# Nine convolution taps on the vector engine, memory rows turned inside the convolution, three steps in another order, and the eight lightest experts four to a round

## The chip, the cores and the metric

The kernel runs as one launch on one core of a Trainium2 chip. The time is device time in microseconds (us) of that core. The five engines (TensorE, VectorE, ScalarE, GpSimd, SyncE) run programs of their own and meet only at semaphores. In the profile's words they are PE (PEld is its weight load), DVE, ACT, POOL and SP; a q behind a name is the engine's queue of DMA issues.

## The reference

One inference step of a decoder layer for 512 prompt rows and 8 sample rows (T = 520 tokens, D = 1024), in float32:

```python
z = rms_norm(x, norm_g) @ w_in                  # 1024 -> 2048: gMLP u, v | conv a, b
a_out = gelu(u) * chunk_spatial_mix(layer_norm(gelu(v)), gm_ws, gm_bs)
glu = cv_a * sigmoid(cv_b)                      # 512 channels
conv = depthwise_causal_conv(glu, conv_w)       # 31 taps
b_out = silu(layer_norm(conv + conv_b))
x = x + concat(a_out, b_out) @ w_out
k, v = rms_norm(mem) @ wk, rms_norm(mem) @ wv   # 256 memory rows, 4 heads
x = x + softmax(q k^T / 16) v @ wo              # q = rms_norm(x) @ wq
...
xt = rms_norm(x)
g = argmax(xt @ router_g + b)                   # top-1 of 4 groups
e = top_2(xt @ router_e[g] + b)                 # top-2 of its 8 experts
out = sum over both of w_e * ((silu(xt @ w1[e]) * (xt @ w3[e])) @ w2[e])
y = rms_norm(x + out)
```

Every expert holds three float32 matrices of 1 MiB each (1024x256, 1024x256, 256x1024).

## The kernel before, in words

It is one function with a hand-written program for each engine. All order is in the code: lists such as `STREAM` (weight loads), `MM_ORDER`, `TV_ORDER` and `TA_ORDER` (who gets the PSUM buffers next) and counting semaphores.

**Dense part.** Activations lie transposed (channels on partitions). A weight slice of 256 columns is loaded by SP into one of four 1 MiB buffers, ScalarE copies it to a rounded high part (`split_h`, L694), VectorE subtracts to a low part (`split_l`, L996), and `project` (L1588 to L1590) makes each product from three matmuls: high x high, low x high, high x low. Two slices' parts fit, so slice n waits for the matmuls of slice n-2. The two PSUM buffers `mm` alternate; a block is free again when VectorE or ScalarE has read it (`mm_used`). The order is: turn x (L1584), 16 blocks of `w_in`, turn the memory rows, the convolution, 8 blocks of keys (`wk`) and 8 of values (`wv`) with the spatial mixing and the layer norm of the convolution between them, 8 of `w_out`, 8 of queries with attention, `wo`, routing.

**Head.** ScalarE scales xT into xH (L715, per k), VectorE makes xL (`moving_l`, L1035), then ScalarE squares the token rows (L720), and through `tok_ms`, a root and `diag` TensorE makes the row of token norms `rs0`, `rs1` (L1645), placed behind block 1. VectorE needs them (`rstd`, L1050) before it can read blocks 0 and 1 out of PSUM (L1095).

**Convolution.** The 512 channels lie as 4 x 128; `conv_taps` (L1694) does all 31 taps on TensorE as 32x32 matmuls with diagonal weights `dw`, 16 for a tap. Ahead of it four groups of memory rows are turned (`mem0` to `mem3`, L1584); each must be read by ScalarE (L752) and VectorE (L1130) before the group two later can be turned, and the taps come last. Behind it ScalarE adds the bias (L770) after it has waited for `m_mean`, the memory norm that VectorE makes once its layer norm of v (L1138) is done.

**Norms between blocks.** `mean(n)` takes two sums out of PSUM (L1007), waits for ScalarE's root, and does a reciprocal (L1009). In the keys the split of slice 11 stands behind `mean(0)` and the scaling of the convolution (L1199); in the queries the split of slice 21 stands behind `mean(1)` and the scaling of the router.

**Experts.** VectorE ranks the 32 experts by their number of rows. Places 0 to 5 are fixed experts, the others follow rank. A round gathers 128 slots (`xe`, GpSimd), turns them, does `hidden` (L1978) with w1 and w3, and `down` (L2006) with w2. A round holds one expert with 128 slots (S) or two with 64 (P), each writing its own rows of PSUM. 28 places lie in 16 fixed rounds; at least one pass of a loop does two more P rounds (places 28 to 31). Weights of an expert go into one of `RING` = 7 slots; SP loads place p+7 into the slot of p: gate and up (L580) after `hid_ready` of p's round, down (L584) after its `y_done`. The down weights of a round are queued ahead of the gates of the next.

## Time and profile before

| | |
|---|---|
| median of 3 runs | 739.23 us (738.95 to 741.88) |
| the profiled execution | 738.92 us, span 737.2 us (1.7 us lie around the span) |
| PE busy | 644.9 us (87%), PEld 471.3 us |
| DVE / ACT / POOL busy | 299.9 / 208.6 / 81.7 us |
| moved by DMA | 179.4 MB, 243 GB/s in the mean |

Busy shares are means over stages that differ much; what holds a stage up is read from the chain of waits and from the timeline of that stage. In the timeline a number in brackets is the idle time ahead of an instruction, with the one that ended it.

### The profile page before, as it was taken

Reading aid. Unit: us, or ns where it says so; the run is one execution under the profiler, and the core shown is the slowest. Engines: PE = TensorE matmul, PEld = TensorE weight load, DVE = VectorE, ACT = ScalarE, POOL = GpSimd, SP = SyncE. Lnnn points to the kernel's source line nnn. Section 1 sums busy time; section 2 is a strip of 40 time slices with the busy share of each in tenths; the row PEclk is TensorE's granted clock in tenths of the full one; section 3 lists DMA queues with packets and bytes.
Section 4 is the critical chain, followed back from the end, with each engine's and each line's share of the span. In section 5 each row is a group of like instructions: output and inputs, shape, how many; then the busy total and the mean of one; then the engine's idle time right before and its main releaser. Section 6 shows DMA issues by size and latency. Waiting matters only on the chain.

```text
span 737.2 us, 11996 instructions
## 1 busy us (share of the span) xinstructions
PE 644.9 (87%) x4939; PEld 471.3 (64%) x4939; DVE 299.9 (41%) x598; ACT 208.6 (28%) x359; POOL 81.7 (11%) x117
## 2 busy tenths in 40 slices
PE   3899997999899998999899996699999999999720
PEld 3899997668799998996678875234333343433210
DVE  3644655808653445578722237111212121121138
ACT  4711423114643433436202132111112121121122
POOL 0000000600000220100101110112121211111100
PEclk8899999999999999999998996699999999999965
DMA  9823130303375432378984649699999999999553
GB/s 289 253 68 135 64 109 1 118 4 90 131 193 141 160 116 91 140 247 291 350 295 190 228 164 418 254 415 420 421 420 419 421 418 419 417 416 417 234 215 142
DMA packets 75470, 179.42 MB, mean 243 GB/s; under 512 B 9710, under 2 KB 56490, under 8 KB 62088
## 3 DMA queue, kind: packets, MB, share of 16 engines
q1 hardware_dynamic: 65868, 163.47, 59.2%
q0 software_dynamic: 6176, 12.76, 4.7%
q10 hardware_dynamic: 3372, 2.42, 1.0%
q8 instruction: 39, 0.64, 0.4%
q14 instruction: 15, 0.12, 0.0%
HBM read 173.85 MB, written 16.66 MB: 258 GB/s over the span
## 4 chain that ended last, share of the span: by engine, by line
PE 75%; DMA 9%; DVE 8%; issue 4%; ACT 2%; SPq 1%; ACTq 1%; DVEq 0%; POOLq 0%
PE ps L1978 15%; PE ps L1588 12%; PE ps L1590 12%; PE ps L1589 12%; PE ps L2006 7%; PE ps L1694 4%; DMA w<-exp_w 4%; PE ps L1584 4%; PE ps L1775 2%; DMA raw<-cache_mem_k 2%; PE ps L1875 1%; DMA xs_rows<-x_sample 1%; PE ps L1712 1%; PE ps L1837 1%; DVE rstd L1009 1%
## 5 line engine op out<-in xcount | busy, mean ns | idle before, releaser
L1588 PE MATMUL ps<-xH,w_h 128*128 128x260 f32 x512 | 150.0, 293 | 9.2 <-DVE xL L1035 5.2
L1589 PE MATMUL ps<-xH,w_l 128*128 128x260 f32 x512 | 146.7, 286 | 0.0
L1590 PE MATMUL ps<-xL,w_h 128*128 128x260 f32 x512 | 146.7, 286 | 0.0
L1978 PE MATMUL ps<-w,xeT 128*64 128x512 f32 (+1 forms) x512 | 129.0, 601 | 3.9 <-DMA w<-exp_w 2.6
L1588 PEld LDWEIGHTS ps<-xH,w_h 128*128 128x128 f32 x512 | 98.7, 193 | 14.6 <-DVE w_l L996 7.7
L1978 PEld LDWEIGHTS ps<-w,xeT 128*64 128x64 f32 (+1 forms) x512 | 44.6, 145 | 86.1 <-issue 84.4
L1589 PEld LDWEIGHTS ps<-xH,w_l 128*128 128x128 f32 x512 | 98.7, 193 | 0.3 <-issue 0.2
L1590 PEld LDWEIGHTS ps<-xL,w_h 128*128 128x128 f32 x512 | 98.6, 193 | 0.0
L996 DVE TENSOR_TENSOR w_l<-raw,w_h 128x2048 fp32r<-128x2048 f32 x28 | 64.1, 2289 | 35.3 <-ACT w_h L694 35.3
L2006 PE MATMUL ps<-w,aT 128*64 128x512 f32 (+1 forms) x256 | 66.0, 599 | 10.5 <-DVE aT L1501 10.5
L694 ACT ACTIVATE w_h<-raw 128x2048 fp32r<-128x2048 f32 x28 | 53.3, 1904 | 19.1 <-PE ps L1590 17.6
L1494 DVE SCALAR_TENSOR_TENSOR gated<-ps,rs_slot,silu 128x256 f32<-128x256 f32 x16 | 7.7, 484 | 111.4 <-ACT silu L935 111.4
L2006 PEld LDWEIGHTS ps<-w,aT 128*64 128x64 f32 (+1 forms) x256 | 20.8, 143 | 43.5 <-issue 30.4
L1588 PE MATMUL ps<-w_h,xH 128*128 128x256 f32 x128 | 37.4, 292 | 4.1 <-DVE w_l L996 3.1
L1508 DVE COPY ye<-ps 128x512 f32<-128x512 f32 x18 | 12.5, 692 | 68.0 <-PE ps L2006 68.0
L935 ACT ACTIVATE silu<-ps,rs_slot 128x256 f32<-128x256 f32 x16 | 7.6, 475 | 102.9 <-PE ps L1978 102.9
L1590 PE MATMUL ps<-w_l,xH 128*128 128x256 f32 x128 | 36.7, 287 | 0.0
L1589 PE MATMUL ps<-w_h,xL 128*128 128x256 f32 x128 | 36.5, 285 | 0.0
L1590 PE MATMUL ps<-cL,w_h 128*128 128x260 f32 x128 | 36.2, 283 | 0.0
L1588 PE MATMUL ps<-cH,w_h 128*128 128x260 f32 x128 | 36.1, 282 | 0.0
L1589 PE MATMUL ps<-cH,w_l 128*128 128x260 f32 x128 | 36.1, 282 | 0.0
L2125 POOL DMA_INDIRECT y_rows<-ye,ids x16 | 16.1, 1009 | 172.6 <-DVE ye L1508 172.6
(332 smaller groups left out, 899.3 us busy)
## 6 DMA issues: line engine op xcount, KB each, us to landing
w<-exp_w SPq DMA_DIRECT2D x96, 1024.0 KB, 21.4
raw<-w_in SPq DMA_DIRECT2D x8, 1024.0 KB, 6.7
raw<-cache_mem_k SPq DMA_DIRECT2D x8, 1024.0 KB, 6.6
raw<-cache_mem_v SPq DMA_DIRECT2D x8, 1024.0 KB, 11.9
raw<-xa_wk SPq DMA_DIRECT2D x4, 1024.0 KB, 5.7
raw<-xa_wv SPq DMA_DIRECT2D x4, 1024.0 KB, 5.4
raw<-xa_wq SPq DMA_DIRECT2D x4, 1024.0 KB, 5.1
raw<-xa_wo SPq DMA_DIRECT2D x4, 1024.0 KB, 5.5
```

The lines of the kernel that those rows point to most:

```text
L694: act.activation(w_h[n % 2][:], slot[:], ACT.Copy).then_inc(h_ready, 1)
L996: dve.tensor_tensor(w_l[n % 2][:], slot[:], w_h[n % 2][:].bitcast(F32), ALU.subtract).then_inc(l_ready, 1)
L1508: dve.tensor_copy(ye[j][:, 512:D], mm[1][:, 1, :]).then_inc(yv_ready, 1)
L1584: return pe.transpose(out, src, ident[0:n, 0:n])
L1588: pe.matmul(out, h1, h2, start=start, stop=False)
L1589: pe.matmul(out, l1, h2, start=False, stop=False)
L1590: return pe.matmul(out, h1, l2, start=False, stop=stop)
L1694: last = pe.matmul(out[r // 2][c * BAND:(c + 1) * BAND, r % 2, :], dw[c // 2][rows, c % 2, k, :], glu[rows, c, k:k + SEQ], start=k == 0, s ...
L1775: last = pe.matmul(out[:, j // 2, (j % 2) * MEM:(j % 2 + 1) * MEM], qT[:, 2 * h + kk, j * P:(j + 1) * P], kT[:, 2 * h + kk, :], start=kk = ...
L1978: last = pe.matmul(mm[0][half, j, :], xeT[j][:, k, half], w13[s][:, :, k, :], start=k == 0, stop=k == KT_D - 1)
L2006: last = pe.matmul(mm[1][half, b, :], aT[:, k, half], w2s[s][:, k, c], start=k == 0, stop=k == 1)
L2125: pool.indirect_dma_start(out=y_rows, out_offset=bass.IndirectOffsetOnAxis(ap=index, axis=0), in_=ye[j][:], in_offset=None, bounds_check=2 ...
```

## The change

Four things. (1) `V_TAPS` = 9 of the 31 taps become 36 VectorE instructions (`part_taps`), dealt out between its steps of `w_in` by `PART_AT` and between the memory rows; TensorE does 22 taps and adds VectorE's partial sum by 16 matmuls with the identity. `mem0` and `mem1` are turned ahead of the taps, `mem2` and `mem3` before the 7th and the 9th tap of TensorE. (2) The token squares go between the copies of x on ScalarE (three) and to VectorE (two); blocks 0 and 1 of `w_in` become one `first_pair` in three passes (high x high as xH comes, low x high, the norm rows, high x low); x is loaded by half, with a semaphore each. (3) The splits of slices 11 and 21 stand ahead of the waits for the root, the router's scaling behind the split of slice 22. (4) The rounds are `PPPSPPPSPQSPQS`: two rounds hold four experts with 32 slots each, 14 fixed rounds instead of 16. The step from rank to slot is written anew for three sizes. The number of experts loaded stays 32: by the reference's routing no expert is over its slots in either version (the eight lightest ranked ones have at most 24 rows).

```diff
-for kind in "PPPSPPSPPSPPSPPP":
+for kind in "PPPSPPPSPQSPQS":
     p = ROUNDS[-1][-1] + 1 if ROUNDS else 0
-    ROUNDS.append((p,) if kind == "S" else (p, p + 1))
+    ROUNDS.append(tuple(range(p, p + {"S": 1, "P": 2, "Q": 4}[kind])))
...
+                if j < 3:
+                    row = x_row(act, j)
+                    act.wait_ge(*((tok_sq, j) if j else (dve_made, 4)))
+                    act.activation(mem_junk[:], row, ACT.Square, accum_out=tok_ss[:, j:j + 1]).then_inc(tok_sq, 1)
...
+                dve.tensor_tensor_reduce(v_junk[0:n], row, row, 1.0, 0.0, ALU.mult, ALU.add,
+                                         tok_ss[0:n, j:j + 1]).then_inc(tok_sq_v, 1)
...
+                if n == 0:
+                    split_l(11)
                 dve.wait_ge(rs_root, n + 1)
                 dve.reciprocal(rstd[:], rstd[:]).then_inc(rs_ready, 1)
...
+            part_todo = [(k, c) for pair in ((0, 1), (2, 3)) for k in range(V_TAPS) for c in pair]
...
+                    src, w = glu[:, c, k:k + SEQ], cols_b[:, k, c:c + 1]
+                    if k == 0:
+                        ins = dve.tensor_scalar(conv[:, c, 0:SEQ], src, w, None, ALU.mult)
+                    else:
+                        dve.wait_ge(part_done, part_last[c])
+                        ins = dve.scalar_tensor_tensor(conv[:, c, 0:SEQ], src, w, conv[:, c, 0:SEQ], ALU.mult, ALU.add)
...
+            PART_AT = {4: 3, 5: 4, 6: 4, 7: 3, 8: 2, 9: 3, 10: 3, 11: 3, 14: 3}
...
             moving_l(7, 32, "xa_g")
+            split_l(21)
             mean(1)
...
+            def first_pair():
+
+                outs = [open_mm(("w_in", m)) for m in range(2)]
...
+                for k in range(8):
+                    pe.wait_ge(xh_ready, k + 1)
+                    for out, c in zip(outs, cols):
+                        for b, tok in enumerate(toks):
+                            pe.matmul(out[:, b, 0:HT], wh[:, k, c], xH[:, k, tok], start=k == 0, stop=False)
+                pe.wait_ge(l_ready, 1)
...
+                token_norms()
...
+            MEM_AT = {V_TAPS + 6: 2, V_TAPS + 8: 3}
...
-                for k in range(TAPS):
+                for k in range(V_TAPS, TAPS):
+                    if k in MEM_AT:
+                        mem_turned(MEM_AT[k])
+                    if k == TAPS - 1:
+                        pe.wait_ge(part_done, 4 * V_TAPS)
+                        for r in range(4):
+                            rows = slice(r * BAND, (r + 1) * BAND)
+                            for c in range(4):
+                                pe.matmul(out[r // 2][c * BAND:(c + 1) * BAND, r % 2, :], ident[rows, rows],
+                                          conv[rows, c, 0:SEQ], start=False, stop=False)
```

What VectorE does at the head, before, behind its copies of x (`w_l_55` is the low part of slice 0, `w_l_56` of slice 1):

```order
L1026 MEMSET glu 128x4x30
L996 TENSOR_TENSOR w_l_55<-raw_51,w_h_53 128x2048
L1035 SCALAR_TENSOR_TENSOR xL<-xT,cols_a,xH 128x520 x8
L1041 TENSOR_SCALAR tok_ss<-tok_ss 128x5
L1043 RECIPROCAL tok_ss<-tok_ss 128x5
L1046 TENSOR_SCALAR diag<-ident,tok_ss 128x128 x4
L1046 TENSOR_SCALAR diag<-ident,tok_ss 8x8
L996 TENSOR_TENSOR w_l_56<-raw_52,w_h_54 128x2048
L1050 COPY rstd<-ps 128x260 x2
```

And now, from the second of its two squares on:

```order
L1059 ISA v_junk,tok_ss<-xs_rows 8x1024
L1059 ISA tok_ss 8x1
L1063 TENSOR_SCALAR tok_ss<-tok_ss 128x5
L1019 TENSOR_TENSOR w_l_55<-raw_51,w_h_53 128x2048
L1072 SCALAR_TENSOR_TENSOR xL<-xT,cols_a,xH 128x520 x5
L1078 RECIPROCAL tok_ss<-tok_ss 128x5
L1081 TENSOR_SCALAR diag<-ident,tok_ss 128x128 x4
L1081 TENSOR_SCALAR diag<-ident,tok_ss 8x8
L1072 SCALAR_TENSOR_TENSOR xL<-xT,cols_a,xH 128x520 x3
L1086 COPY rstd<-ps 128x260 x2
L1019 TENSOR_TENSOR w_l_56<-raw_52,w_h_54 128x2048
```

The norm's reciprocal and `diag` moved between the fifth and the sixth xL, and the split of slice 1 behind the norm rows.

TensorE at the start of the convolution, before (`raw_51` holds the memory rows, 16 turns are the four groups):

```order
L1590 MATMUL ps<-xL,w_h_54 128x260
L1584 MATMUL ps<-ident,raw_51 128x128 x16
L1694 MATMUL ps<-glu,dw_109 32x512 x2
L1694 MATMUL ps<-glu,dw_110 32x512 x2
L1694 MATMUL ps<-glu,dw_109 32x512 x2
```

Now, at the 9th of TensorE's taps, where `mem3` is turned (8 turns stand ahead of the first tap, 4 more ahead of the 7th):

```order
L1794 MATMUL ps<-glu,dw_109 32x512 x2
L1794 MATMUL ps<-glu,dw_110 32x512 x2
L1641 MATMUL ps<-ident,raw_51 128x128 x4
L1794 MATMUL ps<-glu,dw_109 32x512 x2
L1794 MATMUL ps<-glu,dw_110 32x512 x2
```

The taps no longer stand behind the last group of memory rows.

VectorE in the keys, before (`w_l_56` is slice 11):

```order
L1152 COPY kT<-ps 128x512
L1007 TENSOR_SCALAR rstd<-ps 128x260 x2
L1009 RECIPROCAL rstd<-rstd 128x520
L1199 TENSOR_TENSOR cLf<-cLf,rstd 128x2080
L996 TENSOR_TENSOR w_l_56<-raw_51,w_h_54 128x2048
L1152 COPY kT<-ps 128x512
L996 TENSOR_TENSOR w_l_55<-raw_52,w_h_53 128x2048
```

And now:

```order
L1211 COPY kT<-ps 128x512
L1030 TENSOR_SCALAR rstd<-ps 128x260 x2
L1019 TENSOR_TENSOR w_l_56<-raw_51,w_h_54 128x2048
L1034 RECIPROCAL rstd<-rstd 128x520
L1259 TENSOR_TENSOR cLf<-cLf,rstd 128x2080
L1211 COPY kT<-ps 128x512
L1019 TENSOR_TENSOR w_l_55<-raw_52,w_h_53 128x2048
```

The split of slice 11 moved ahead of the reciprocal; slice 12 kept its place.

## Rows read from the trace of the kernel before

**Rows 1.** The page, the span in 40 slices of 18.43 us: bytes moved.

```profile
GB/s 289 253 68 135 64 109 1 118 4 90 131 193 141 160 116 91 140 247 291 350 295 190 228 164 418 254 415 420 421 420 419 421 418 419 417 416 417 234 215 142
```

**Rows 2.** Windows table: busy us of each engine, then clock, DMA share, GB/s.

```profile
60.00:100.00 40.00, 40.00 (x337) 39.96 (x336) 20.77 (x27) 12.41 (x12) 0.00 (x0) 1.00 0.23 80
```

**Rows 3.** The chain that ended last, expert stage: start, us, what.

```profile
468.63 8.67 PE ps L1978 x32
...
483.15 6.87 PE ps L1978 x32
...
649.75 6.89 PE ps L1978 x32
...
659.27 31.71 DMA w<-exp_w
...
691.12 7.10 PE ps L1978 x32
```

**Rows 4.** Timeline of SyncE's queue: start, us to issue, line, count.

```profile
477.49 2.10 SPq L580 DMA_DIRECT2D w<-exp_w  x4
...
579.87 6.54 SPq L580 DMA_DIRECT2D w<-exp_w  x4
...
656.88 8.62 SPq L580 DMA_DIRECT2D w<-exp_w  x4
```

**Rows 5.** Groups by form: partitions x elements, count, busy us, mean ns.

```profile
L1694 PE MATMUL ps<-glu,dw 32*32 32x512 f32 x992 | 33.3, 612 | 0.1
...
L1035 DVE SCALAR_TENSOR_TENSOR xL<-xT,cols_a,xH 128x520 fp32r<-128x520 f32 x16 | 11.8, 775 | 0.1
...
L1837 PE MATMUL ps<-raw,s_pT 128*32 128x256 f32 x128 | 7.1, 380 | 0.0
```

**Rows 6.** Timeline of the head: start, us, engine, line, idle before it.

```profile
15.79 5.05 ACT L715 ACTIVATE xH<-xT,cols_a 128x520 fp32r<-128x520 f32 x8
...
19.03 0.56 PE L1588 MATMUL ps<-xH,w_h 128*128 128x260 f32 x1 [5.17 <-DVE xL L1035]
...
24.37 0.42 PE L1588 MATMUL ps<-xH,w_h 128*128 128x260 f32 x1
...
24.89 0.28 PE L1588 MATMUL ps<-xH,w_h 128*128 128x260 f32 x1
...
36.08 0.36 PE L1588 MATMUL ps<-xH,w_h 128*128 128x260 f32 x1 [1.35 <-DVE glu L1095]
```

**Rows 7.** Timeline of TensorE, from the last input block to the first tap.

```profile
121.86 1.04 PE L1584 MATMUL ps<-ident,raw 128*128 128x128 f32 x8
126.78 1.90 PE L1584 MATMUL ps<-ident,raw 128*128 128x128 f32 x8 [3.88 <-DVE xL L1130]
128.61 1.16 PE L1694 MATMUL ps<-glu,dw 32*32 32x512 f32 x16
```

**Rows 8.** Timeline of the convolution's end and the first key block.

```profile
144.39 0.20 ACT L761 ACTIVATE m_ss<-m_ss 128x2 f32<-128x2 f32 x1 [12.62 <-DVE m_ss L1143]
...
161.99 2.66 ACT L770 ACTIVATE cLf<-ps,cols_a 128x512 f32<-128x512 f32 x4 [17.39 <-PE ps L1694]
...
163.44 0.36 PE L1588 MATMUL ps<-w_h,xH 128*128 128x256 f32 x1 [0.98 <-ACTq L775]
```

**Rows 9.** Timeline of the keys: split, first block behind it, copies of ScalarE.

```profile
195.01 2.29 DVE L996 TENSOR_TENSOR w_l<-raw,w_h 128x2048 fp32r<-128x2048 f32 x1
...
197.35 0.39 PE L1588 MATMUL ps<-w_h,xH 128*128 128x256 f32 x1 [3.08 <-DVE w_l L996]
...
200.33 2.20 ACT L796 ACTIVATE cH<-cLf 128x520 fp32r<-128x520 f32 x4
```

**Rows 10.** Timeline of the queries, TensorE alone.

```profile
289.03 0.36 PE L1588 MATMUL ps<-xH,w_h 128*128 128x260 f32 x1 [2.29 <-DVE cHf L1225]
```

**Rows 11.** Timeline of VectorE in the routing.

```profile
447.68 0.24 DVE L1399 TENSOR_SCALAR at_rank<-ps,part_no 32x32 f32<-32x32 f32 x1 [0.52 <-PE ps L1937]
...
453.04 0.18 DVE L1436 CAST slot_f<-slot_i 128x20 f32<-128x20 int32 x1
```

More of the change, by code:

```diff
@@ L42 @@
 PAST = TAPS - 1
+V_TAPS = 9
+PE_TAPS = TAPS - V_TAPS
 MEM = 256
@@ L82, in runs_of @@
     while at < len(values):
-        n = 1
-        while at + n < len(values) and values[at + n] == values[at] + n:
+        n, step = 1, values[at + 1] - values[at] if at + 1 < len(values) else 0
+        while at + n < len(values) and values[at + n] == values[at + n - 1] + step:
             n += 1
-        out.append((at, n, values[at]))
+        out.append((at, n, values[at], step))
         at += n
+    return out
     return out
@@ L376, in trunk_kernel @@
         rs_root = sem("rs_root")
+        x_landed = [sem(f"x_landed{j}") for j in range(NT - 1)]
         tok_sq = sem("tok_sq")
+        tok_sq_v = sem("tok_sq_v")
         tok_ms = sem("tok_ms")
@@ L537, in load @@
                         sp.dma_start(dst[g * BAND:(g + 1) * BAND, 4:8, :], rows).then_inc(landed[HOME[c]], 16)
+                elif kind == "x":
+                    for t in range(2):
+                        sp.dma_start(dst[:, t:t + 1, :], src[:, t:t + 1, :]).then_inc(x_landed[2 * i + t], 16)
                 else:
@@ L1432, in _ @@
[L1432 to L1435 removed]
+            dve.wait_ge(block_ready, 1)
+            link(dve.tensor_copy(first[:], mm[1][:, 0, 0:2 * EXPERTS]))
+            cap_b = each(first[:, EXPERTS:2 * EXPERTS]).broadcast_to([P, NT, EXPERTS])
@@ new lines, in _ @@
+            link(dve.tensor_tensor(ptmp[:], ptmp[:], each(first[:, 0:EXPERTS]).broadcast_to([P, NT, EXPERTS]), ALU.add))
+            link(dve.tensor_tensor(ptmp[:], ptmp[:], e_all[:].rearrange("p t g e -> p t (g e)"), ALU.add))
+            for_two = ptmp[:].rearrange("p (o t) e -> p o t e", o=1).broadcast_to([P, 2, NT, EXPERTS])
+            link(dve.tensor_tensor(wtmp[:], who[:], for_two, ALU.mult))
+            link(dve.tensor_reduce(place[:], wtmp[:], AX_X, ALU.add))
+            link(dve.tensor_scalar(place_i[:], place[:], float(OVER_FIRST), None, ALU.add))
@@ new lines, in first_pair @@
+            def first_pair():
+                outs = [open_mm(("w_in", m)) for m in range(2)]
+                wh = w_h[0][:].rearrange("p (k c) -> p k c", k=8)
+                wl = w_l[0][:].rearrange("p (k c) -> p k c", k=8)
+                cols = [slice(m * P, (m + 1) * P) for m in range(2)]
+                toks = [slice(b * HT, (b + 1) * HT) for b in range(2)]
+                pe.wait_ge(h_ready, 1)
+                for k in range(8):
[4 more added lines that the diff above has]
+                pe.wait_ge(l_ready, 1)
+                for out, c in zip(outs, cols):
+                    for k in range(8):
+                        for b, tok in enumerate(toks):
+                            pe.matmul(out[:, b, 0:HT], wl[:, k, c], xH[:, k, tok], start=False, stop=False)
+                token_norms()
+                for out, c in zip(outs, cols):
+                    for k in range(8):
+                        pe.wait_ge(xl_ready, k + 1)
+                        for b, tok in enumerate(toks):
+                            last = pe.matmul(out[:, b, 0:HT], wh[:, k, c], xL[:, k, tok], start=False, stop=k == 7)
+                    last.then_inc(mm_ready, 1)
@@ L1648, in _ @@
+            first_pair()
+            for m in range(2, 16):
+                project("w_in", m, xH, xL)
                 if m == 3:
@@ L1674, in _, with mem_turned @@
                         last.then_inc(tv_ready, 1)
-            slot = raw_in(pe, ("mem", 0))
-            for i in range(4):
+            def mem_turned(i):
+                slot = raw_in(pe, ("mem", 0))
                 out = open_tv(f"mem{i}")
```

180 lines of the change are left out of this document (99 added, 81 removed).

## The prediction, made before the changed kernel ran

> **What bounds the kernel now.** I read the chain of waits first, then the bytes by slice, SyncE's queue, and the timeline where TensorE waits. Two stages with different limits show.
>
> Up to the routing TensorE is the limit: nearly every piece of the chain there is its own, and what it does not do, or what it stops waiting for, comes off the time. Its waits are few: at the head it starts the first products at 19.03 and block 2 at 36.08 [rows 6]; between the last block of `w_in` and the first tap lie 128.61 - 121.86 = 6.7 us [rows 7]; one split in the keys costs 3.08 us of idling [rows 9], one in the queries 2.29 us [rows 10].
>
> From the second half of the routing on, the limit is the stream of expert weights. The first seven experts fill the slots; slot 0 is free again when the first `hidden` ends, and SyncE issues at 477.49 [rows 4]. From there the bytes stand at 415 to 421 GB/s in every slice up to 676 us [rows 1], and SyncE's issues stretch from 2.10 to 6.54 and 8.62 us for four [rows 4], as they do when a queue takes no more. TensorE runs beside it: from 483.15 to 649.75 lie 13 rounds, 12.8 us each [rows 3]. The last gate and up weights land at 659.27 + 31.71 = 690.98 and the last `hidden` starts at 691.12 [rows 3]; at TensorE's own pace that round would have come 649.75 + 3 x 12.8 = 688.2. So rounds and bytes are nearly in balance, and the bytes end last.
>
> **The change, part by part.** All on the clock of before; a step that ends earlier moves everything behind it, since nothing behind has a time of its own.
>
> *Head.* ScalarE's xH starts at 15.79, one k every 0.63 us (5.05 / 8) [rows 6]. The first pass of the pair needs only that: it starts at about 16.6 instead of 19.03. It has 32 matmuls. At 24.37 the rows still last 0.42, at 24.89 0.28 us [rows 6]: the granted clock went from 1.2 to 2.4 GHz 5.6 us after the start, and starts go from 0.22 to 0.12 us apart. Started at 16.6 it would change at 22.2: 26 matmuls by then, 6 more to 22.9; the second pass of 32 to 26.8, the norm rows (12 starts at 0.12 us, 1.4) to 28.2, the third pass to 32.1. VectorE's list: squares of two row tiles (1024 columns, an estimate of 1.3 us each from 520 in 0.775 [rows 5]), split of slice 0, five xL, reciprocal and `diag` near 24, three xL by 26.2, norm rows at 28.7, split of slice 1 to 31.0, block 0 read at 31.7. So block 2 starts at 32.1 instead of 36.08: **-4.0**. Bounds: -1.5 if the squares between ScalarE's copies push xH by a us and the split of slice 1 comes late too; -5.5 if the clock rises sooner.
>
> *Taps.* 31 taps take 33.3 us [rows 5], 1.07 each: nine less are -9.6. The partial sum's 16 matmuls have a tap's form: +1.1. The taps start behind `mem1`, at 122.9 (121.86 + 1.04 [rows 7]), instead of 128.61, and the 8 later turns (0.9) stay between them: -4.8. The end comes then at 148.4, and ScalarE's bias is not held by the taps alone any more. It waits for `m_mean`, which came at 144.39 in a VectorE list that started behind `mem3` [rows 8]. `mem3` is now turned behind eight taps, by 132.3 instead of 128.68, and partial taps stand among the groups, so `m_mean` comes some 4.3 us later, near 148.7: +0.3. Sum **-13.0** for the start of the keys (163.44 [rows 8]). Bounds: -9 (a VectorE list 4 us later than I have it) and -13.5.
>
> VectorE pays 36 x about 0.62 us (a 520-column instruction of this kind lasts 0.775 and the next starts before it ends [rows 5]) = 22 us. It is busy 20.77 of 40 us in `w_in` [rows 2]; from block 4 to block 15 are some 60 us, so 29 are free, for 28 instructions (17 us). I went through the list block by block: with four taps in a block the next split ends 7.0 us behind the block, its successor is wanted 11.5 behind. Hidden, price 0. If that cover were gone, each us that VectorE is late costs TensorE one.
>
> The GPSIMD Engine Reference of the Trainium skill (1. Specifications) says that GpSimd shares its memory interfaces with VectorE when an instruction there has two inputs in SBUF, as these have. It would hurt under GpSimd's work; here GpSimd is busy 0.00 us [rows 2], so the rule has no hold.
>
> The turns inside the taps are another matter: the array goes from 32x32 tiles to whole and back twice. At the one such change of before, turns end at 128.68 (126.78 + 1.90) and the first tap starts at 128.61 [rows 7]: nothing lost. The Trainium skill, TensorEngine Tiling (Array Packing), Key Properties, says that changing the mode drains the engine; with a drain as long as a tap's matmul (0.612 us [rows 5], an estimate) four changes are 2.4 us and the time would be 721.1. I go by the row.
>
> *Keys.* Slice 11's split (195.01 to 197.30 [rows 9]) stands before the reciprocal and ends near 191; its block starts at 194.4 instead of 197.35. But ScalarE is busy for the convolution until 200.33 + 2.20 = 202.5 [rows 9], so block wk6 is read out at 203.0 and wv0 starts there, against 205.3 before: **-2.2**. Bounds: 0 (TensorE idles 2.5 us there and falls back to half clock) and -4.5.
>
> *Queries.* Slice 21 is split while the norm is made; queries 0 are read right after the reciprocal, block 2 starts at about 286.7 instead of 289.03 [rows 10]: **-2.3**, bounds -1 and -2.5. The router's scaling (under 0.5 us) lies before queries 2, TensorE in a block.
>
> *Routing.* From `at_rank` to `slot_f` are 453.04 - 447.68 = 5.4 us, some 25 small instructions [rows 11]. The new text has fewer in a row, but three of 160 columns: I add up 5.0, **-0.5**, bounds -1.2 and +0.5. GpSimd writes 33 instead of 18 runs of the tables, 19 us before they are read: 0.
>
> *Rounds.* 73 loads of 1 MiB land from 477.49 to 690.98: 2.92 us each. The first `hidden` is as it was, so the stream starts, and the last gate lands, at the same place of this clock. With 67 loads the gates of 28 and 29 are in at 673.4; with 56 those of 26, at 641.3; with 37 those of 19, at 585.7, where the first group of four is due. Fewer rounds only make TensorE wait: some 17 us before the second group (the round ahead of it ends at 624.1), 4.9 us before the last round (673.4 + 12.8 = 686.2 to 691.0). The freed slots are asked for 17 us and more before the stream gets to them, so it has no hole. **0** for the two rounds less. But after a wait TensorE comes back slow: the first `hidden`, behind the routing, lasts 8.67 against 6.87 [rows 3]. The last one now has 4.9 us of idling before it instead of 3: **+1.8**; bounds 0 and +5.
>
> Sum: -4.0 - 13.0 - 2.2 - 2.3 - 0.5 + 1.8 = **-20.2 us**. The profiled execution had 738.92, 0.3 under the median: 738.9 - 20.2 = **718.7 us**.
>
> **Rivals.**
> - *Small gains lost* (0.18). Only the taps pay; head, keys and queries give back what they save at the next wait: 738.9 - 13.0 + 1.8 = 727.7, with half of them 723. For: behind slice 11 ScalarE is already the next one late. Against: behind the others TensorE has whole blocks before it.
> - *VectorE becomes the limit in `w_in`* (0.10). If a partial tap cost 1.28 us, two blocks with seven taps would need 15 us in 11.5; three such pairs put some 10 us back: about 729. Only then; at 0.8 us it still fits.
> - *TensorE was the limit of the expert stage* (0.05). Then two rounds less are 2 x 12.8 us more: 693. Against: 31.71 us from issue to landing, and the flat GB/s. The Trainium skill, DMA: Bandwidth & Descriptors, Specifications, has a limit of 358 GB/s from memory for one core and 435 for the ports; the trace's 420 is above the first, so the measurement decides.
> - *Slower: groups of four don't run side by side* (0.04). Four tiles of 32 columns one after the other make `hidden` 27.5 instead of 6.9 and `down` 14.6 instead of 3.7: 31.5 us more a group. The second group would start at 624.1 + 31.5 = 655.6, the last round three rounds and 31.5 us later, at 725.5 instead of 691.0: 718.7 + 34.5 - 1.8 = 751.4. It ends slower than before once a group costs 25 us more, since the last round must then start 22 us late. Against: L1837 has four tiles of 32 columns, 128 records in 7.1 us [rows 5], 55 ns for 256 columns each, a quarter of what they need one by one.
> - *Four drains around the turned memory rows* (0.1): 718.7 + 2.4 = 721.1, if each change of tile size holds TensorE for as long as one tap's matmul lasts; the row on the one change of before shows no hold.
> - The rest (0.53) is the forecast, by itself 714 to 723.
>
> **How the numbers follow.** 718.7 is the likeliest case. The bounds of its terms together reach from 712 to 731; taking in most of the first rival, the range 712 to 728 leaves out the stream rival, the slow group and part of the VectorE case, under 2 in 10. Faster by over 0.5% (3.7 us, about what a measurement of this kernel can tell from no change): 0.94; within it 0.02; slower 0.04.
>
> **What the profile will show.** Block 2 near 32; first tap near 118.9, 4 us earlier by the head and 5.7 by the turns; the keys' first block near 146.5; VectorE's instruction of a partial tap at 0.7 us; 420 GB/s from the first `hidden` to some 669 us; TensorE idle before the second group of four. Wrong would be: TensorE waiting for VectorE between the blocks of `w_in`, bytes under 400 GB/s in the expert stage, or a `hidden` of four longer than 9 us.

## The result and the profile after

The changed kernel takes **719.82 us** (median of 4 runs, 718.43 to 721.74); the kernel before, on the same chip, 739.49 us (738.95 to 741.88). The ratio is 0.973 with a 95% interval of 0.9707 to 0.9753: 19.7 us less, where 20.2 had been predicted (718.7, range 712 to 728). The profiled execution has 718.43 us and a span of 716.6; TensorE's mean granted clock is 0.933 where it was 0.945.

The page shows the bytes of the 40 slices (17.92 us each) and the granted clock in tenths:

```profile
PEclk8999999999999999999989985999999899699975
...
GB/s 294 268 144 61 105 73 2 121 80 138 156 127 228 66 118 119 236 238 355 290 354 118 118 378 312 364 419 419 420 419 421 418 421 420 418 421 399 185 236 133
```

418 to 421 GB/s stand from slice 27 to slice 36, as in [rows 1]. The clock has two new dips, at its 32nd and 35th digit, where TensorE waits for the weights of the two groups of four.

The head, as a timeline of ScalarE and TensorE (start, us, engine and line, operands, count, idling before it and what ended it):

```profile
15.55 5.05 ACT L742 ACTIVATE xH<-xT,cols_a 128x520 fp32r<-128x520 f32 x8
...
16.42 5.74 PE L1717 MATMUL ps<-xH,w_h 128*128 128x260 f32 x32 [2.79 <-ACT xH L742]
...
21.99 4.01 PE L1722 MATMUL ps<-xH,w_l 128*128 128x260 f32 x32
...
25.84 1.59 PE L1701 MATMUL ps<-diag,ones 128*128 128x128 f32 x12
...
27.36 4.09 PE L1728 MATMUL ps<-xL,w_h 128*128 128x260 f32 x32
31.28 0.28 PE L1645 MATMUL ps<-xH,w_h 128*128 128x260 f32 x1
```

The first pass starts at 16.42, 0.87 us behind xH's first start, and block 2 at 31.28, 4.8 us sooner than in [rows 6]. Of these, 0.2 are an earlier start of xH (15.55 against 15.79), which lies between 15.15 and 16.64 in the runs below, whatever they change. At the end of `w_in` the lead is 4.9 us.

TensorE through the convolution, and then the first key block:

```profile
116.98 1.03 PE L1641 MATMUL ps<-ident,raw 128*128 128x128 f32 x8
117.99 6.57 PE L1794 MATMUL ps<-glu,dw 32*32 32x512 f32 x192
124.49 0.66 PE L1641 MATMUL ps<-ident,raw 128*128 128x128 f32 x4
125.07 2.35 PE L1794 MATMUL ps<-glu,dw 32*32 32x512 f32 x64
127.35 0.66 PE L1641 MATMUL ps<-ident,raw 128*128 128x128 f32 x4
127.94 11.92 PE L1794 MATMUL ps<-glu,dw 32*32 32x512 f32 x358
140.92 1.86 PE L1794 MATMUL ps<-glu,dw 32*32 32x512 f32 x45 [1.05 <-issue]
...
145.25 0.44 PE L1802 MATMUL ps<-cs,ident 128*32 128x8 f32 x32
146.68 0.35 PE L1645 MATMUL ps<-w_h,xH 128*128 128x256 f32 x1 [0.99 <-ACTq L798]
```

Block 15's turns start at 116.98 and the first tap follows at 117.99, 1.0 us later, against 6.75 in [rows 7]. Between the blocks of `w_in` TensorE waits for VectorE once, 1.2 us for `wsT`, as it did before; no product of a block waits. The taps end at 145.32. One row is new: 1.05 us ahead of 140.92 in which TensorE waits for nothing that the profile shows ("issue"). The keys start at 146.68 (163.44 in [rows 8]), ScalarE's bias 1.46 ahead of them, right behind the taps. VectorE's partial taps as a group (count | busy us, mean ns):

```profile
L1120 DVE SCALAR_TENSOR_TENSOR cLf<-glu,cols_b,cLf 128x512 f32<-128x512 f32 x32 | 22.3, 746 | 0.0
```

32 multiply-adds of 746 ns, each starting some 0.67 us behind the last; the four first ones are plain multiplies of 0.48.

In the keys, ScalarE's list, and the value block that waits for it:

```profile
177.50 1.91 ACT L717 ACTIVATE w_h<-raw 128x2048 fp32r<-128x2048 f32 x1
...
179.43 1.28 ACT L815 ACT_TABLE_LOAD   x1
...
180.72 2.96 ACT L815 ACTIVATE cLf<-cLf,cols_a 128x520 f32<-128x520 f32 x4
...
183.59 2.20 ACT L819 ACTIVATE cH<-cLf 128x520 fp32r<-128x520 f32 x4
...
185.69 0.81 ACT L832 ACTIVATE zt<-ps,m_ss 128x256 f32<-128x256 f32 x2
...
186.29 0.35 PE L1645 MATMUL ps<-w_h,xH 128*128 128x256 f32 x1 [2.64 <-ACT zt L832]
```

Block wk6 is read out by the first of the two copies at 185.69; TensorE idles 2.64 us for it, and 1.1 us after it has started again its clock falls to half. A table by stretches (busy us and counts of the engines, then clock, DMA share, GB/s):

```profile
187.00:190.60 3.60, 3.60 (x21) 3.60 (x20) 2.25 (x1) 1.32 (x1) 0.00 (x0) 0.55 0.44 110
367.00:371.50 4.50, 4.50 (x22) 4.49 (x21) 0.25 (x2) 0.00 (x0) 0.00 (x0) 0.50 1.02 413
```

17 steps between 187.3 and 190.9 take 0.21 instead of 0.12 us. The second line is the start of the attention's output projection, behind the small products that end in `con`; it runs at half clock too. The expert stage, from the chain that ended last:

```profile
446.62 8.84 PE ps L2080 x32
...
461.31 6.87 PE ps L2080 x32
...
639.57 29.34 DMA w<-exp_w
...
669.05 8.57 PE ps L2080 x32
```

The last gate lands at 639.57 + 29.34 = 668.91, that is 222.29 us behind the first `hidden`'s start; before, 690.98 - 468.63 = 222.35 [rows 3]. Two rounds fewer changed the stream by nothing. TensorE's waits in that stage:

```profile
PE ps L2080 <- DMA w<-exp_w: 23.0, 4, 14.7
```

Before:

```profile
PE ps L1978 <- DMA w<-exp_w: 2.6, 2, 2.2
```

23.0 us in four waits, where 2.6 in two were, are what the saved rounds became. The longest stands ahead of the second group of four:

```profile
567.93 9.59 PE L2080 MATMUL ps<-w,xeT 128*32 128x512 f32 x64 [4.22 <-DMA w<-exp_w]
...
623.83 8.96 PE L2080 MATMUL ps<-w,xeT 128*32 128x512 f32 x64 [14.71 <-DMA w<-exp_w]
```

### The profile page after: what moved, and what is told of

It is laid out like the page before. It is cut to its first block, busy times and chain, and to the rows that moved or that the text cites. A ratio compares the mean times of both kernels' runs of the same rounds, so it can differ in the third digit from the quotient of the medians.

```text
span 716.6 us, 11489 instructions
## 1 busy us (share of the span) xinstructions
PE 616.9 (86%) x4667; PEld 454.4 (63%) x4667; DVE 318.1 (44%) x625; ACT 201.2 (28%) x343; POOL 79.4 (11%) x130
## 4 chain that ended last, share of the span: by engine, by line
PE 68%; DMA 17%; DVE 5%; SPq 4%; issue 3%; ACT 2%; ACTq 1%; POOLq 0%; DVEq 0%
DMA w<-exp_w 13%; PE ps L1645 12%; PE ps L1647 12%; PE ps L1646 12%; PE ps L2080 11%; PE ps L2108 4%; SPq L603 3%; PE ps L1794 3%; PE ps L1641 3%; PE ps L1875 2%; DMA raw<-cache_mem_k 2%; PE ps L1975 1%; DMA xs_rows<-x_sample 1%; PE ps L1812 1%; PE ps L1937 1%
## 5 line engine op out<-in xcount | busy, mean ns | idle before, releaser
L2080 PE MATMUL ps<-w,xeT 128*64 128x512 f32 (+2 forms) x512 | 120.9, 646 | 24.4 <-DMA w<-exp_w 23.0
L1645 PE MATMUL ps<-xH,w_h 128*128 128x260 f32 x480 | 139.3, 290 | 0.4 <-DVE xL L1327 0.2
L1647 PE MATMUL ps<-xL,w_h 128*128 128x260 f32 x480 | 136.5, 284 | 0.0
L1646 PE MATMUL ps<-xH,w_l 128*128 128x260 f32 x480 | 136.5, 284 | 0.0
L2080 PEld LDWEIGHTS ps<-w,xeT 128*64 128x64 f32 (+2 forms) x512 | 40.8, 146 | 103.0 <-issue 101.2
L1645 PEld LDWEIGHTS ps<-xH,w_h 128*128 128x128 f32 x480 | 91.4, 190 | 5.5 <-issue 4.9
L1646 PEld LDWEIGHTS ps<-xH,w_l 128*128 128x128 f32 x480 | 91.3, 190 | 0.2
L1647 PEld LDWEIGHTS ps<-xL,w_h 128*128 128x128 f32 x480 | 91.4, 190 | 0.0
L2108 PE MATMUL ps<-w,aT 128*64 128x512 f32 (+2 forms) x256 | 58.6, 598 | 9.3 <-DVE aT L1558 9.3
L2108 PEld LDWEIGHTS ps<-w,aT 128*64 128x64 f32 (+2 forms) x256 | 18.4, 136 | 38.6 <-issue 27.1
```

The source lines that it names most:

```text
L1645: pe.matmul(out, h1, h2, start=start, stop=False)
L1646: pe.matmul(out, l1, h2, start=False, stop=False)
L1647: return pe.matmul(out, h1, l2, start=False, stop=stop)
L2080: last = pe.matmul(mm[0][half, j, :], xeT[j][:, k, half], w13[s][:, :, k, :], start=k == 0, stop=k == KT_D - 1)
L2108: last = pe.matmul(mm[1][half, b, :], aT[:, k, half], w2s[s][:, k, c], start=k == 0, stop=k == 1)
```

## The experiments

All are compared with runs of the kernel before on the same chip. "The changed kernel" has 719.82 us and 0.973. Where single microseconds are told apart I go by the distance between two landmarks of the profile, since one stretch varies by itself: the load of the samples' cached keys (DMA raw<-cache_mem_k on the chain) took 13.56 us before, 11.89 in the changed kernel, and 11.92 to 13.47 in the runs below, whatever they change.

**Sixteen rounds again** (rounds16)

```diff
-for kind in "PPPSPPPSPQSPQS":
+for kind in "PPPSPPSPPSPPSPPP":
```

> The changed kernel with the 16 fixed rounds of before (no group of four), all else as changed. If the bytes are the limit of the expert stage, the last gate and up weights land 222.3 us after the first hidden starts, as in both profiles (690.98 - 468.63 and 668.91 - 446.62), TensorE's longest wait there falls from 14.7 us to under 3, and only the last hidden is cheaper (7.1 instead of 8.6 us, since less idling stands ahead of it): 718.3 us, 1.5 less than the changed kernel. If TensorE is the limit, two rounds more cost 2 x 12.8 = 25.6 us: 745.

719.06 us, ratio 0.9702 (0.9674 to 0.9731): the same as the changed kernel. The last gate lands at 673.67, 222.66 us behind the first `hidden`. TensorE's row of the last round:

```profile
673.81 7.09 PE L2080 MATMUL ps<-w,xeT 128*64 128x512 f32 x32 [1.87 <-DMA w<-exp_w]
```

It waits 1.87 instead of 2.74 us and then takes 7.09 instead of 8.57. In the whole stage TensorE waits 2.4 us for weights, not 23.0. TensorE is not the limit of this stage, and the fewer rounds of the change bring nothing; by these rows they cost 1.5 us at the end. The medians, 0.8 us apart, are too near each other to show so little.

**All memory rows ahead of the taps** (mem_first)

```diff
-            MEM_AT = {V_TAPS + 6: 2, V_TAPS + 8: 3}
+            MEM_AT = {}
...
                 mem_turned(1)
+                mem_turned(2)
+                mem_turned(3)
```

(and `part_taps(0 ...)` instead of `part_taps(2 ...)` between the groups)

> The changed kernel with all four memory rows turned ahead of the first tap; VectorE's six partial taps between their groups come behind the last group. My theory: TensorE waits for VectorE and ScalarE between the turns as before, the first tap starts 5.7 us later (123.7 instead of 118.0) and 8 turns (0.9 us) no longer stand among the taps: 4.8 us more, 724.6. If every change of the array's tile size holds TensorE for one tap's matmul (0.6 us), four changes go away: only 2.4 us more, 722.2. If VectorE's list had been the limit behind the taps, it would be the same as the changed kernel, 719.8.

724.52 us, ratio 0.9782 (0.9752 to 0.9811).

```profile
116.40 1.03 PE L1641 MATMUL ps<-ident,raw 128*128 128x128 f32 x8
121.35 1.87 PE L1641 MATMUL ps<-ident,raw 128*128 128x128 f32 x8 [3.92 <-DVE xL L1188]
123.15 1.16 PE L1796 MATMUL ps<-glu,dw 32*32 32x512 f32 x16
```

The wait for VectorE's xL is back (3.92 us) and the first tap starts 6.75 us behind block 15's turns, exactly as before the change. From there to the last tap's end lie 32.72 us against 28.34 in the changed kernel: 4.4 more, 5.1 when each one's "issue" gap (0.32 and 1.05) is taken off. At the start of the keys 3.6 us are left of it, since the wait behind the taps is 0.20 instead of 0.99 us; the medians are 4.7 apart. So the new place of the turns is worth 4 to 5 us. The drain rival, by which only 2.4 would be lost, falls. The changed kernel's own rows agree: 192 records of the trace (32 a tap, so six taps) take 6.50 us, the four turns 0.58.

**Slice 11's split where it was** (keys_old)

```diff
-                if n == 0:
-                    split_l(11)
                 dve.wait_ge(rs_root, n + 1)
...
-                if n != 10:
-                    split_l(n + 1)
+                split_l(n + 1)
```

> The changed kernel with slice 11's split behind the keys' reciprocal again, as before. What the trace of the changed kernel shows: ScalarE's list (split of slice 12, table load, silu, copies) lets the first value block start at 186.3 whatever comes earlier, so TensorE idles ahead of slice 11's block instead of behind it: 0 to 0.3 us more, 719.9. What the prediction said: 2.2 us more, 722.0.

719.76 us, ratio 0.9732 (0.97 to 0.9764). From the first key block to the first block of `w_out` lie 64.68 us; 64.42 in the changed kernel. The time is that of the changed kernel (719.82), and the idling is only at another place:

```profile
179.62 0.58 PE L1642 MATMUL ps<-w_h,xH 128*128 128x256 f32 x1 [3.08 <-DVE w_l L1019]
```

3.08 us ahead of slice 11's block and half clock behind it, instead of 2.64 ahead of the value block and half clock there. The move is worth 0.26 us.

**ScalarE's order in the keys** (keys_act)

```diff
-                if n == 11:
-                    act.wait_ge(conv_norm, 1)
...
                     act.activation(dst, mm[MM_AT[key] % 2][:, 0, 0:MEM], ACT.Copy, scale=m_ss[:, t:t + 1]).then_inc(mm_used, 1)
+                    if (n, t) == (11, 0):
+                        act.wait_ge(conv_norm, 1)
+                        for r in range(4):
+                            act.activation(conv[:, r, :], conv[:, r, :], ACT.Silu, scale=column("cv_g", r),
+                                           bias=column("cv_b", r)).then_inc(conv_out, 1)
+                    if (n, t) == (12, 0):
+                        for r in range(4):
+                            act.wait_ge(conv_out, 4 + r + 1)
+                            act.activation(cH[:, 4 + r, :], conv[:, r, :], ACT.Copy).then_inc(xh_ready, 1)
```

> The changed kernel with ScalarE's silu put behind its read of key block 6, and the copies of the silu's result behind its read of value block 0. If ScalarE's order alone sets the start of the first value block, that block starts at about 183.3 instead of 186.3 and TensorE, idle for less than a us, stays at 2.4 GHz, where it now runs 21 steps of 0.21 instead of 0.12 us: 3.0 + 2.0 = 5 us less, 714.8. If another engine is the next one late (VectorE's scaling, or the split of slice 13, which has to end by 189.4), under 2 us less: 718 or more.

717.90 us, ratio 0.9703 (0.9672 to 0.9734): 1.9 us under the changed kernel, where 5 were expected if ScalarE's order were all, and under 2 if another engine were next. The same stretch has 61.67 us: 2.75 less. The clock stays up (clock column 1.00):

```profile
183.30:190.60 7.30, 6.31 (x52) 5.86 (x50) 2.85 (x2) 7.30 (x11) 0.00 (x0) 1.00 0.63 177
```

But ScalarE's read of wk6 waits for a store of keys until 181.46, and its split of slice 13 comes at 186.47 and VectorE's half of it ends at 190.7, 1.1 us behind the turned keys (189.57):

```profile
181.46 0.48 ACT L824 ACTIVATE zt<-ps,m_ss 128x256 f32<-128x256 f32 x1 [2.48 <-DMA out_mem_k_prompt<-zt]
...
186.47 1.90 ACT L717 ACTIVATE w_h<-raw 128x2048 fp32r<-128x2048 f32 x1
```

Between the last turned keys and `w_out` 0.83 us are lost again. ScalarE's order was the cause; the split is the next one late.

**Slice 21's split where it was** (queries_old)

```diff
-            split_l(21)
             mean(1)
...
+            split_l(21)
             queries(0)
             queries(1)
```

(and `split_h(21)` on ScalarE behind the root in the same way)

> The changed kernel with slice 21's split behind the queries' norm again, on ScalarE and VectorE, as before. By the prediction (and by 15.09 against 12.57 us from the sums to the first scores in the two profiles) TensorE idles 2.3 us ahead of block 2 again: 2.5 us more, 722.3. If ScalarE's exponentials or the sample rows were next, it would be the same, 719.8.

723.59 us, ratio 0.9785 (0.9764 to 0.9806). From the first block of `w_out` to the first scores lie 66.39 us, 64.25 in the changed kernel: 2.14 more, of which TensorE waits

```profile
PE ps L1645 <- DVE cHf L1288: 1.9, 1, 1.9
```

for the split. The forecast of 2.3 holds; the rest of the difference of the two spans (721.8 and 716.6) lies in the head (1.0), in the "issue" gap of the taps (0.5), between the queries and the norms' product (0.9) and behind the start of the first `hidden` (0.5), where nothing was changed. The medians, 3.8 apart, hold such differences too.

**Spare matmuls in TensorE's waits** (warm)

```diff
+            def fill(out, count):
+
+                for _ in range(count):
+                    pe.matmul(out[:, 0:P], ones[:], ident[:], start=True, stop=True)
...
+            pe.wait_ge(ta_used, len(TA_ORDER))
             pe.wait_ge(who_ready, 1)
...
+            fill(ta[1], 2)
...
+            fill(ta[1], 18)
...
+            fill(ta[1], 22)
...
+                fill(ta[1], 10)
                 slots = [(2, it + 5), (3, it + 5)]
```

> The changed kernel with spare matmuls (ones by identity, 128 columns, result read by nobody) put into TensorE's waits: 2 ahead of the ranks' products and 18 behind them, 22 between the routing list's product and the first turned rows, 10 ahead of the last hidden. If the granted clock alone makes these pieces slow and the weights' stream starts when the first hidden ends: the list's product 4.99 to 2.6 us, the turns 1.95 to 1.16, the first hidden 8.84 to 6.87, and all behind them 5.2 us earlier; the last hidden 8.57 to 7.1: 6.7 less in all, 713.1. If the first hidden is slow because weights land beside it, it stays at 8.8 and the sum is 3 less: 716.6. If the clock doesn't come back although the engine is busy, the 40 spare matmuls take 0.43 instead of 0.21 us each and some 7 us are lost: 727.

719.76 us, ratio 0.9732 (0.9716 to 0.9748): no gain, where 6.7 us less were expected.

```profile
424.86 1.65 PE L2031 MATMUL ps<-both,ones 128*128 128x32 f32 x10 [0.86 <-ACT x L936]
...
438.70 2.72 PE L2063 MATMUL ps<-col_hot,row_hot 128*128 128x52 f32 x20
...
449.57 8.78 PE L2089 MATMUL ps<-w,xeT 128*64 128x512 f32 x32 [1.31 <-ACT xeT L950]
...
671.92 7.09 PE L2089 MATMUL ps<-w,xeT 128*64 128x512 f32 x32 [0.32 <-DMA w<-exp_w]
```

Two parts came out in opposite ways. The last `hidden` takes 7.09 instead of 8.57 us behind its ten spare matmuls: its slowness was the clock. In the routing the wait that I had added let TensorE idle 0.86 us, the clock fell at 425.8, some 3 us of work sooner in TensorE's list than without it, and the spare matmuls ran at half clock. The list's product took 2.72 instead of 4.99 us but started 5.2 us later, counted from the norms' product. The first `hidden`, behind 1.31 us of idling, fell back to half clock 0.1 us after its start and took 8.78. From the norms' product to its end 45.2 us went by, 42.7 in the changed kernel: the routing lost 2.5 us, more than the last `hidden` gained.

**Twelve taps on VectorE** (taps12)

```diff
-V_TAPS = 9
+V_TAPS = 12
...
-            PART_AT = {4: 3, 5: 4, 6: 4, 7: 3, 8: 2, 9: 3, 10: 3, 11: 3, 14: 3}
+            PART_AT = {4: 3, 5: 5, 6: 4, 7: 5, 8: 3, 9: 5, 10: 3, 11: 4, 14: 4}
...
-            part_taps(2)
+            part_taps(4)
```

(and the steps of `m_mean` behind the second row tile of v)

> The changed kernel with twelve taps on VectorE instead of nine (48 partial taps at 0.67 us; 28 were ahead of block 15, now 36; m_mean is made behind the second row tile of v so that it doesn't hold the bias). If VectorE still has room: three taps of 1.07 us less on TensorE, 3.2 less, 716.6. If nine was near VectorE's limit, TensorE waits for VectorE between the blocks of w_in (a split or a read-out that ends late) and the time stays or rises: 719.8 or more.

716.98 us, ratio 0.9712 (0.9688 to 0.9737): 2.8 us under the changed kernel, and 3.2 were expected. VectorE still has room, no block of `w_in` waits for it, and the taps end 3.4 us sooner. In the profiled execution, which took 720.24 us, the keys then take most of it back:

```profile
140.83 1.13 PE L1795 MATMUL ps<-glu,dw 32*32 32x512 f32 x26 [1.22 <-issue]
...
143.42 0.55 PE L1646 MATMUL ps<-w_h,xH 128*128 128x256 f32 x1 [1.09 <-ACTq L798]
```

```profile
143.50:149.30 5.80, 5.80 (x27) 5.80 (x28) 3.98 (x4) 3.42 (x4) 3.56 (x3) 0.50 0.00 0
```

Behind two short waits (1.22 and 1.09 us) the first key blocks run at half clock, 29 steps of 0.21 instead of 0.12 us: 2.7 us. In the changed kernel the same two waits (1.05 and 0.99) left the clock at 2.4 GHz. Four of the six executions took only 716.6 to 717.1 us, with a mean granted clock of 0.931 to 0.935 instead of this one's 0.927. So the loss in the keys is shown for this execution; that the four escaped it is a guess, since they have no trace. (Over the changed kernel's, this execution's span is 1.9 us longer; the cached keys' load, 13.39 us here, is 1.5 of that.)

**The waits filled with more care** (warm2)

The wait for the copied rows stands behind the ranks' product; 2, 18, 26 and 5 spare matmuls in the routing, 8 ahead of `con`, 10 ahead of the last `hidden`.

> The changed kernel with spare matmuls again, placed by what the run before showed: TensorE's wait for the copied rows stands behind the ranks' product, where it waits anyway (ahead of the counts it cost 0.86 us of idling and the clock), 26 instead of 22 behind the list's product, 5 between the turned rows and the first hidden, 8 ahead of the three products that end in con, 10 ahead of the last hidden. By the clock theory: list product 4.99 to 2.7, turns 1.95 to 1.16, first hidden 8.84 to 6.9 (5.0 together), the first half unit of the output projection behind con 2.0 less, the last hidden 1.5 less: 8.5 less, 711.3. If the small products of the routing (32 columns) let the clock fall whatever stands around them, the routing gains nothing: 3.5 less, 716.3.

717.82 us, ratio 0.9684 (0.9646 to 0.9723), where 711.3 was expected, or 716.3 if the routing gained nothing. The first `hidden` takes 7.09 instead of 8.84, the last one 7.1. But the 18 spare matmuls ran at half clock again, since the clock fell inside the routing's products of 32 columns ahead of them; the list's product started 3.0 us later and was 2.3 shorter. The eight ahead of `con` ran at half clock as well, behind products of 4 columns, and only moved the slow stretch. From the norms' product to the first `hidden`'s end: 42.7 us in the changed kernel, 42.4 here.

**Everything together, with nine and twelve taps** (all9, all12, all12b)

all9 is warm2 with ScalarE's silu spread over the key and value blocks (one row behind wk6, two ahead of value block 0, one behind it, the copies behind value block 2), five spare matmuls between taps and keys, and 5 and 11 in the head. all12 adds the twelve taps. all12b has 11 instead of 18 behind the ranks' product.

> warm2, and with it ScalarE's new order in the keys (silu of one row behind key block 6, of two ahead of value block 0, one behind it, the copies behind value block 2, VectorE's second halves behind slice 14's split), 5 spare matmuls between the taps and the keys, 5 and 11 in the head. Keys: 3.6 less as in the earlier run with ScalarE's order alone, and 0.8 more if the split of slice 13 isn't late any more; head: 1.0 less, since the first pass then goes at the pace of ScalarE's xH (0.63 us a k) and not at half clock. Together 5.4 less than warm2: 705.9. If only the idling moves to another place, it is no better than warm2.

> all9 with twelve taps on VectorE. In the earlier run with twelve taps the taps ended 3.4 us sooner and 29 steps of the first key blocks then ran at 1.2 GHz (0.21 instead of 0.12 us each, 2.7 us), behind two waits of 1.2 and 1.1 us. If the clock took that gain, the 5 spare matmuls keep it: 3.2 less than all9, 702.7. If VectorE or GpSimd (row tiles of v, made later) is the limit, it equals all9: 706.

> all12 with 11 instead of 18 spare matmuls behind the ranks' products. In all12 those 18 took 6.9 us (most at half clock, since the clock fell in the small products just ahead of them) and the routing list's product came 23.4 us behind the norms' product, 3.0 later than in the changed kernel. By the clock theory 11 of them take 4.7 us at half clock, the list's product starts 2 us sooner, and TensorE stays busy through it, so that the first hidden still takes 7.1 us: 2 less than all12, 707. If 11 aren't enough to bring the clock back in time, the list's product takes 5.0 instead of 2.7 us again: the same as all12, 709.

all9: 710.71 us, ratio 0.9603 (0.9568 to 0.9638). That is 7.1 less than warm2, where 5.4 had been expected, but 4.8 over the 705.9 named, since warm2 itself had come out 6.5 too slow. all12: 709.06, 0.9574 (0.9537 to 0.9612): 1.7 less than all9, half of the 3.2 expected, with intervals that overlap. all12b: **707.72**, 0.9561 (0.9534 to 0.9589), 12 us less than the changed kernel. These runs change several things at once, so only the stretches tell them apart. All in all 10.9 us lie between the profiled spans of all12b and the changed kernel: 4.4 in the keys, 3.2 in the taps, 1.5 in the last `hidden`, 1.0 in the routing with the first `hidden`, 0.9 up to the end of `w_in`. In all9's keys the stretch to `w_out` is 60.01 us (64.42), so 4.4 less, as expected with slice 13's split in time. From the first pass to block 15's end, the head's spare matmuls included, it has 99.84 us (100.56), 0.7 less where 1.0 was expected. With twelve taps the first key blocks stay at full clock (all12b):

```profile
142.60:148.40 5.80, 5.80 (x51) 5.67 (x49) 4.28 (x4) 3.35 (x4) 3.85 (x3) 1.00 0.01 3
```

and the keys start 3.4 us sooner than with nine. In all12b the routing list's product comes 1.8 us sooner than in all12, but the first `hidden` starts at the same distance (34.6 us behind the norms' product). In all12 the 26 spare matmuls behind the list's product held TensorE until then, so they lay on the chain themselves. In all12b VectorE reads the list out only behind its own count of the loops, and the gather behind it took 4.93 us, 3.48 in the changed kernel:

```profile
429.53 0.14 DVE more L1530
...
429.98 0.10 DVE ids L1535
...
431.16 4.93 DMA xe<-x_rows,gids
```

The expectation of 2 us less is not shown to hold: 1.3 lie between the medians, with intervals that overlap.

**Fourteen taps** (all14)

> all12b with fourteen taps on VectorE (56 partial taps, 42 ahead of block 15). By the row tiles of v: they are normalised behind the partial taps, GpSimd's last scaling ended 1.5 us ahead of TensorE's first read of it in the run with twelve, and now ends 1.3 us later while TensorE comes 2.1 us sooner: TensorE waits 2 us there and nothing is gained, 707 as all12b. If VectorE still had room everywhere it would be 2.1 less, 705; if VectorE is late between the blocks of w_in as well, more than all12b.

709.94 us, ratio 0.9577 (0.955 to 0.9603): nothing gained over all12b, as expected; the intervals overlap, so that it is slower isn't shown. The profiled execution is the slowest of the five (713.60; the lowest is 708.39). In it the limit is where it was expected, only larger:

```profile
PE ps L1651 <- POOL v_s L2202: 3.9, 1, 3.9
```

GpSimd and VectorE beside it:

```profile
142.63 1.33 POOL L2200 TENSOR_TENSOR v_tok<-v_tok,ln_g 128x512 f32<-128x512 f32 x1 [0.43 <-DVE v_tok L1206]
144.03 3.94 POOL L2202 TENSOR_TENSOR v_tok<-v_tok,ln_b 128x512 f32<-128x512 f32 x1
147.94 1.26 POOL L2200 TENSOR_TENSOR v_s<-v_s,ln_g 8x512 f32<-8x512 f32 x1
```

```profile
144.57 2.27 DVE L1028 TENSOR_TENSOR w_l<-raw,w_h 128x2048 fp32r<-128x2048 f32 x1
```

GpSimd's addition of `ln_b` to a row tile took 3.94 us at 144.03, where the same instruction takes 1.26 to 1.28 on the three tiles ahead, while VectorE split slice 9 in its usual 2.27, an instruction with two inputs in SBUF. In taps12 and all12b the split was the one that lasted longer beside GpSimd (2.93 and 3.26 instead of 2.28), and GpSimd's instruction kept its 1.28. The GPSIMD Engine Reference of the Trainium skill (1. Specifications) has this as a shared interface; by that rule, which gives no size, the two of them compete here, and the traces agree.

## Why the prediction was right

The time was right within 1.1 us, in part by luck. The profiled execution's 20.6 us of span divide like this, each against the step of the prediction:

- *Head*, -4.0 said, -4.8 to block 2 and -4.9 to the end of `w_in`. The clock rose 3.6 us after the first pass began, not 5.6, which the bound of -5.5 had foreseen.
- *Taps*, -13.0 said, -11.9 measured (163.44 to 146.68 less the head's 4.9). 5.7 came from the start behind `mem1` (4.8 net of the turns was said; mem_first gives 4.4 to 5.1), the rest from nine taps less and the identity. The term was too large mostly by the 1.05 us of "issue", which no row of before could show. The bias held by `m_mean`, +0.3, did not happen, and not because `m_mean` was early: on the clock of before (4.9 us of head added back) it came at 148.5, as forecast (148.7), but the taps ended at 150.2 instead of 148.4, behind it. A partial tap costs VectorE 0.67 us, not 0.62, and stayed hidden.
- *Keys*, -2.2 said, -0.4 measured (64.85 to 64.42 us from the first key block to `w_out`), of which the split's move is 0.26 (keys_old). **This step failed.** "Block wk6 is read out at 203.0 and wv0 starts there, against 205.3 before: -2.2" had the start right: wv0 starts 39.6 us behind the first key block, before 41.6, 2.0 sooner. What it left out of the sum is that TensorE now idles 2.64 us just ahead of it, so that wv0 and the block behind it take 7.3 us to the next turned keys, before 5.8: 1.5 go back to the clock. Before, the same loss lay ahead of wv0, behind the wait of 3.08 us [rows 9], inside the 205.3. I had this as the bound of 0 and booked the full gain; it should have been the term. The cure was in ScalarE's list (keys_act with 2.75 us; in all9, with the next split in time too, 4.4).
- *Queries*, -2.3 said, -2.5 measured (66.77 to 64.25 us from `w_out` to the first scores), 2.1 by queries_old.
- *Routing*, -0.5 said, -0.5 measured from the norms' product to the first `hidden` (34.36 to 33.89).
- *Rounds*, 0 said, 0 measured (222.35 to 222.29), and rounds16 shows it from the other side. The waits ahead of the groups of four were said to be 17 us for the second and are 14.7.
- *Tail*, +1.8 said, +1.5 measured, and warm shows that it is the clock.
- *Not in the sum*: the cached keys' load took 1.7 us less in this execution. The later runs show that it varies by as much without a cause in the code. The steps above add up to -18.7 us, 1.5 short of the forecast; that the spans differ by 20.6 is this load, and that is luck. Whether it helped the medians too, whose 19.7 is nearer to the forecast than the steps, no run can tell.

Of the rivals, "small gains lost" was right for the keys alone. VectorE was no limit in `w_in` at nine taps, nor at twelve; it is, with GpSimd, at fourteen, and behind the taps, not between the blocks. "Groups of four don't run side by side" fell: the first such `hidden` takes 9.59 us and the second 8.96 against 27.5 for one after the other. The first is over the 9 us that I had named as a sign, but both started behind idling (4.22 and 14.71 us) and ran their first 5.1 and 3.8 us at half clock. Without that, by the same rows, both would take 7.0 us, as a round of two does. The rival that TensorE is the limit of the expert stage fell with rounds16: 745 by that rival, 719.06 measured.

What stays partly open is the "issue" gap. It appears in every run but the one before the change, with 0.70 to 1.83 us, and 0.32 with the memory rows first. It keeps its place in TensorE's own list of instructions: at the 307th matmul of the taps with nine and, the identity's 16 counted, at the same number with twelve; at the 291st where 16 spare matmuls stand in the head (all9 to all14, the fourteen taps' gap behind their last one); and in mem_first at the 179th, 128 places sooner in the list. That points to the supply of instructions, and a second view bears it out. The profile's DMA view has a queue named `instruction`, which moves 0.02 MB at a time. Just ahead of the gap one such load comes late, behind 6 us in which loads of weight slices keep the DMA engines busy (in the changed kernel a share of 0.87 to 1.09 from 133 to 139 us), and the gap ends the same time after it in all thirteen profiles that have one, 2.4 to 2.6 us. Five of them:

| run | the load ahead, then this load | gap | gap ends |
|---|---|---|---|
| the changed kernel | 131.3, 138.3 | 1.05 | 140.92 |
| rounds16 | 131.5, 139.6 | 1.83 | 142.02 |
| keys_old | 130.5, 137.55 | 0.87 | 139.93 |
| mem_first | 127.3, 133.75 | 0.32 | 136.26 |
| all12b | 129.35, 136.3 | 0.95 | 138.81 |

The view doesn't say for which engine a load is, and no run here moves the weights' loads to test it. What the rows show is that the later the instruction load, the longer the gap.

## What to carry to other kernels

Before a removed wait is booked as a gain, ask which engine is the next one late at the same place and whether TensorE then still idles long enough to come back at half clock: here one split's move was worth 0.26 us, the reorder of the engine behind it 2.75 in the same stretch, and both together with the next late split 4.4. Where bytes are the limit of a stage, fewer rounds of matmuls turn into waiting, and what they change is the clock after the wait. Short waits near each other deserve spare matmuls whose result nobody reads, but only in the wait itself: each of them that runs at half clock and outlasts the wait costs what it should save.

## What the runs showed of the hardware

- Two waits of 1.22 and 1.09 us with 1.5 us of work between them cost the clock for almost 7 us (taps12), while 1.05 and 0.99 us with 4.8 us of work between them did not (the changed kernel), nor did 1.55 and 0.99 us (queries_old) or 1.83 and 0.99 us (rounds16).
- TensorE fell to half clock in the routing's products of 32 columns, with waits of 0.1 to 0.4 us between them, in every run (in warm just ahead of them); spare matmuls behind them brought it back 6.8 us (all12b) to 10.2 us (all9) after it fell, and without them it stayed down for 24 us, until 3.6 us into the first `hidden`. A clock that was brought back lasted through 0.60 and 1.31 us of idling and fell 0.1 us into the next product (warm).
- Changing between 32x32 tiles and the whole array cost nothing that the rows show (under 0.1 us a change). The Trainium skill, TensorEngine Tiling (Array Packing), Key Properties, speaks of a drain at each change and gives no length; four such changes stand in the changed kernel, and their rows leave no room for one of more than 0.1 us.
- Where an SBUF instruction of GpSimd and a split of VectorE ran at the same time, one of the two kept its length and the other lasted longer: GpSimd's 3.94 instead of 1.28 us in all14, VectorE's 2.93 and 3.26 instead of 2.28 in taps12 and all12b.
- Four 32-column tiles ran side by side: a `hidden` of 64 matmuls for four experts took 8.96 us, of which 3.8 at half clock; one of two experts with 32 matmuls took 7.04 at full clock.
